# Attention units key group by key group, two weight splits moved, one opening half and one store moved, in a two-part transformer kernel

## The reference

```python
xn = rms_norm(h, mix_norm[l])
proj = einsum("bsd,dp->bsp", xn, w_in[l]) + b_in[l]
q, k, v, cb, cc, cx, ga, gc = split(proj, splits)
attn = sliding_window_attention(q, k, v, sinks[l])       # 8 heads of 64, 2 key groups, blocks of 128
conv = cb * causal_depthwise_conv(cc * cx, conv_w[l])
merged = sigmoid(ga) * (attn @ w_attn_branch) + sigmoid(gc) * (conv @ w_conv_branch)
h = h + merged @ w_out
hn = rms_norm(h, ffn_norm[l])                            # then up, conv, silu(gate)*val, down
...
return rms_norm_2(x, final_gain)                         # after the two hybrid layers
```

## Time and profile before

| | us |
|---|---|
| three runs, median | 1186.59 |
| the profiled execution | 1185.57 |
| its span, first to last instruction | 1183.8 |
| TensorE busy | 1172.0 |
| VectorE busy | 896.3 |
| ScalarE busy | 577.1 |
| GpSimd busy | 246.5 |

### The profile page before, as it was taken

The page is one execution under the profiler, slowest core; times in us unless marked ns, Lnnn a source line. Parts: engine busy times, 40 slices in busy tenths (PEclk is TensorE's granted clock), DMA queues, the critical chain, the costliest instruction groups (busy, mean ns, idle before and its releaser), DMA issues.

```text
span 1183.8 us, 14982 instructions
## 1 busy us (share of the span) xinstructions
PE 1172.0 (99%) x5539; PEld 983.4 (83%) x5539; DVE 896.3 (76%) x1482; ACT 577.1 (49%) x972; POOL 246.5 (21%) x223
## 2 busy tenths in 40 slices
PE   9999999999999999999999999999999999999997
PEld 7887788888888888888888888899888888898886
DVE  6889855656776487546776788997897878998876
ACT  6677623324343243325444477764335577753432
POOL 0220399931100000000003602101502311112200
PEclk9999999999999999999999999999999999999999
DMA  6455533333331533233332347663223376663521
GB/s 197 128 170 170 158 90 102 94 98 98 125 94 54 155 90 101 78 111 103 89 107 76 120 134 224 195 175 92 72 72 107 107 205 178 190 185 116 143 89 72
DMA packets 216717, 146.81 MB, mean 124 GB/s; under 512 B 6250, under 2 KB 205380, under 8 KB 216516
## 3 DMA queue, kind: packets, MB, share of 16 engines
q1 hardware_dynamic: 216628, 145.86, 42.3%
q10 hardware_dynamic: 16, 0.00, 0.0%
HBM read 127.49 MB, written 18.35 MB: 123 GB/s over the span
## 4 chain that ended last, share of the span: by engine, by line
PE 87%; DVE 7%; ACT 3%; issue 2%; DMA 1%; POOL 0%; DVEq 0%; SPq 0%; ACTq 0%
PE ps L191 86%; ACT a_p L161 1%; DVE tmp L164 1%; DVE wlo L164 1%; DVE a_p L178 1%; DVE a_pd L182 1%; DVE x1h L167 1%; DVE a_zc L167 0%; ACT whi L161 0%; DMA raw<-in_w_in_dram 0%; DMA xtm<-in_x_dram 0%; DVE smx L164 0%; ACT x1h L161 0%; PE ps L194 0%; DVE a_pt L164 0%
## 5 line engine op out<-in xcount | busy, mean ns | idle before, releaser
L161 ACT ACTIVATE whi<-raw 128x1024 fp32r<-128x1024 f32 (+2 forms) x199 | 206.9, 1045 | 293.5 <-PE ps L191 282.4
L164 DVE TENSOR_TENSOR wlo<-raw,whi 128x1024 fp32r<-128x1024 f32 (+2 forms) x193 | 252.1, 1311 | 43.7 <-ACT whi L161 43.2
L191 PE MATMUL ps<-x0h,whi 128*128 128x512 f32 x1008 | 254.8, 391 | 1.2 <-ACT whi L161 1.2
L191 PE MATMUL ps<-x0h,wlo 128*128 128x512 f32 x1008 | 254.4, 391 | 0.0
L191 PE MATMUL ps<-x0l,whi 128*128 128x512 f32 x1008 | 254.1, 390 | 0.0
L191 PEld LDWEIGHTS ps<-x0h,whi 128*128 128x128 f32 x1008 | 187.4, 188 | 39.6 <-ACT whi L161 1.5
L191 PEld LDWEIGHTS ps<-x0l,whi 128*128 128x128 f32 x1008 | 188.0, 188 | 38.8 <-DVE x0l L167 0.2
L191 PEld LDWEIGHTS ps<-x0h,wlo 128*128 128x128 f32 x1008 | 187.9, 188 | 38.4
L164 POOL TENSOR_TENSOR sums<-sums,sq 128x512 f32<-128x512 f32 x28 | 43.0, 1549 | 446.2 <-ACT sq L161 446.2
L191 PE MATMUL ps<-x1h,wlo 128*128 128x512 f32 x304 | 82.1, 389 | 0.0
L191 PE MATMUL ps<-x1l,whi 128*128 128x512 f32 x304 | 82.1, 389 | 0.0
(11 more groups left out here) (213 smaller groups left out, 1636.4 us busy)
## 6 DMA issues: line engine op xcount, KB each, us to landing
raw<-in_w_in_dram SPq DMA_DIRECT2D x98, 512.0 KB, 4.1
raw<-in_w_up_dram SPq DMA_DIRECT2D x44, 512.0 KB, 3.8
raw<-in_w_out_dram SPq DMA_DIRECT2D x24, 512.0 KB, 3.6
turned<-b_pd SPq DMA_DIRECT2D x16, 640.0 KB, 3.5
raw<-in_w_down_dram SPq DMA_DIRECT2D x16, 512.0 KB, 3.7
b_px<-turned SPq DMA_DIRECT2D x32, 160.0 KB, 3.4
b_p<-turned SPq DMA_DIRECT2D x32, 160.0 KB, 3.6
turned_a<-a_pd SPq DMA_DIRECT2D x6, 512.0 KB, 2.6
```

The source lines that it names most:

```text
L161: return AC.put(lambda e: e.activation(o, i, func, **kw), after, AC, 1)
L164: return on.put(lambda e: e.tensor_tensor(o, a, b, op), after, on, 1)
L191: return PE.put(lambda e: e.matmul(o, l, r, start=start, stop=stop), after, PE if mark else None, 1)
```

## The change

Four edits:
- Low halves of the convolution's cx and cb tiles go to GpSimd for j = 2 and 3; before for j = 0, 1 and 2. So tiles 6, 8, 9 and 11 move to VectorE, 15 and 17 to GpSimd, 12 and 14 stay there.
- In the opening the high half of the second feature tile is written by VectorE, and the low half of the first one comes behind it in VectorE's queue.
- The attention units are put on the agenda one query product sooner, all blocks of key group 0 and then those of group 1, at steps 3, 8, 12, 17, 21, 26, 30, 35 from there. The output bank and the DRAM buffer alternate by block instead of by group. The turning of the values uses bank 5 instead of 3.
- The first half of the last rows is stored from ScalarE's queue.

```diff
-                plan_fm(win, m, on_pool=j < 3 and n != 1)
+                plan_fm(win, m, on_pool=j > 1 and n != 1)
...
-            X0.th[k] = act(hi, PS[bank][:, :], scale=MIX(k), after=[tp, t_mix])
-            X0.tl[k] = stt(lo, PS[bank][:, :], MIX(k), f32(hi), ALU.mult, ALU.subtract, after=[tp, X0.th[k]])
+            if k == 1:
+                X0.th[k] = ts(hi, PS[bank][:, :], MIX(k), None, ALU.mult, after=[tp, t_mix])
+            else:
+                X0.th[k] = act(hi, PS[bank][:, :], scale=MIX(k), after=[tp, t_mix])
+
+            def low():
+                X0.tl[k] = stt(lo, PS[bank][:, :], MIX(k), f32(hi), ALU.mult, ALU.subtract, after=[tp, X0.th[k]])
+
+            if k:
+                if k == 1:
+                    lows.pop()()
+                low()
+            else:
+                lows.append(low)
...
-            free = claim(3)
+            free = claim(5)
...
-            u = (2 * n + g) % 2
+            u = n % 2
...
-            if j == 2:
-                for i, (n, g) in enumerate((n, g) for n in range(4) for g in range(2)):
-                    later(3 + 4 * i, unit_a(g, n))
+            if j == 1:
+                for i in range(8):
+                    later(3 + (9 * i + 1) // 2, unit_a(i // 4, i % 4))
...
-                t_done = dma(out[0][128 * t:128 * t + 128, 0:512], ob[:, t, 0:512], d_out, after=tf)
+                t_done = dma(out[0][128 * t:128 * t + 128, 0:512], ob[:, t, 0:512], d_out, after=tf, on=AC)
```

More of the change, by code:

```diff
@@ L574, in x_features @@
             return tp, rest
-        rests = {}
+        rests, lows = {}, []
         for c in range(4):
@@ L710, in evac_v @@
             yield 4
-            free = claim(3)
+            free = claim(5)
             for b in range(4):
-                tp = tr(PS[3][:, 128 * b:128 * b + 128], t[:, 128 * b:128 * b + 128], IDENT,
+                tp = tr(PS[5][:, 128 * b:128 * b + 128], t[:, 128 * b:128 * b + 128], IDENT,
                         after=[a, free], mark=b == 3)
@@ L716, in evac_v @@
             yield 1
-            src = PS[3][:, :].rearrange("p (b g d) -> p g b d", b=4, g=2)
+            src = PS[5][:, :].rearrange("p (b g d) -> p g b d", b=4, g=2)
             for g in range(2):
@@ L723, in evac_v @@
             vv_tok.extend([th, tl])
-            bank_free[3] = [th, tl]
+            bank_free[5] = [th, tl]
         def evac_q(j):
```

## The result

The kernel after takes 1192.33 us (median of six runs, 1191.32 to 1194.42), the kernel before 1186.19 in the runs beside it (1185.67 to 1187.21). The ratio is 1.0052, 95% interval 1.0039 to 1.0065: slower by 6.1 us, where +1.2 was forecast, and outside the range. The profiled execution took 1192.26 us, 6.7 more than that of before; its span is 1190.5.

A forecast was written before the change was run, and what follows sets the result against it. The prediction took VectorE's queue, not TensorE, to set the attention stage's end. It summed +1.4 (stage) + 0 - 0.2 (last rows) = +1.2 us on a 1186.59 us median to 1187.8 us, range 1184.0 to 1191.0.

The forecast's parts named there:

- The first unit's scores: Attention stage, step 3: TensorE waits for the second query tile's low halves, due at 44.0, losing 3.6 us (2.4 to 3.8).
- third query tile's low halves: Sign on VectorE in the attention stage: these low halves return to 0.77 us each.
- Waits for a_pt remain after 100 us: Sign on TensorE late in the attention stage: waits for the turned probabilities remain, 2 to 5 us in all.
- The tail: Storing the last rows: the second issue starts earlier with the first on ScalarE, -0.2 us (-0.48 to +0.33).
- three waits, not four: Attention stage before the change: TensorE was said to wait four times for a_pt between 33 and 125 us, 3.3 us in all.
- So the stage ends 1.4 us later.: Attention stage: VectorE's queue at the sixth unit's low half, 2.44 - 3.46 + 2.4 = +1.4 us (-0.5 to +3.2).
- the late waits' 4.1: Attention stage before: TensorE's waits for a_pt cost 1.76 + 2.35 = 4.1 us, the most the stage could gain.
- The term that was left to a rival: the clock: First unit: the gap drops TensorE's clock, two steps cost +3.6 us on top of the forecast, 1191.4 us; chance 0.08.
- a clock below 1.00 near 44 us: Sign near the first unit: the forecast is wrong if the granted clock falls below 1.00 there.
- GpSimd's remaining splits all hit: Rival, attention stage: all four GpSimd splits stretch VectorE's two-input operations, +4.5 us there, 1190.9 us; chance 0.28.
- x of 1.2: VectorE's loss beside each of two new GpSimd splits: 1.2 us, the mean of four seen, between 0 and 2.13.
- nothing for the opening: Opening: moving a high half from ScalarE to VectorE was costed at nothing, bounds -0.35 to +0.35 us.

The follow-up runs named there:

- gap filled: The kernel after with nine extra matmuls, result unused, ahead of the second pair of the first unit's waiting scores: 1190.35 us, ratio 1.0039.
- units at 6 + 4i: The kernel after with the first unit started three steps later and units 4 steps apart: 1187.70 us, ratio 1.0009.
- opening filled: The kernel before with two extra matmuls, result unused, ahead of the first weight product: 1186.43 us, ratio 1.0000.
- after with the old opening: The kernel after with the opening of before: 1191.12 us, ratio 1.0043.
- units alone: The kernel before with only the new schedule, bank and buffer of the attention units: 1189.97 us, ratio 1.0029.
- opening only: The kernel before with the opening edit alone: 1186.33 us, ratio 1.0005.
- nothing on GpSimd: The kernel after with all low halves of the convolution's tiles on VectorE: 1189.16 us, ratio 1.0026.
- units from step 5: The kernel before with after's units at steps 5 to 34 and GpSimd splitting only tiles 6, 11, 12 and 14: 1184.17 us, ratio 0.9986.

## Why the prediction was wrong

**What held.** The first unit's scores lost 3.68 us against a forecast of 3.6, the low halves being done at 45.11, or 43.87 without the opening's shift, against 44.0. The third query tile's low halves are back at 0.77 each. Waits for a_pt remain after 100 us, 3.6 us in all. The tail is worth nothing: the issue came sooner as worked out, but the two transfers then took longer. The opening edit costs nothing measurable by itself. One reading was off without effect: the earlier trace rows show three waits, not four.

**The step that failed: "So the stage ends 1.4 us later."** The forecast took VectorE's queue as what sets the end, as if its operations stood at fixed times, and let the first unit's 3.6 us vanish in the late waits' 4.1. But VectorE's queue is itself tied to TensorE: each scaling waits for a product. While TensorE stood still VectorE, rid of its two stretched low halves, got ahead, and then it waited 1.98 us for the delayed fourth query product (52.80). The chain of waits runs over TensorE for 13.95 us from 45.25 on, and VectorE fell behind afresh over the next units. So the first wait and the late waits add: rest 0.03 in the kernel after, the same when 1.6 us are given back early (gap filled), and only 0.8 more when the first unit's 5.3 are taken away (units at 6 + 4i). The chain of before had misled: it leaves TensorE out, but by little. The scaling of a convolution product comes at 58.77 us, 0.8 us after TensorE had gone on to what follows (57.97), and in the same kernel with its opening filled the chain runs over TensorE right up to that product. A TensorE that is 5 us late could hardly hide there. The line of VectorE's timeline in the kernel before:

```profile
58.77 0.68 DVE L164 TENSOR_TENSOR tmp<-ps,rb 128x512 f32<-128x512 f32 x1
```

**The term that was left to a rival: the clock.** The forecast gave 0.08 to a fall at the first unit. It fell in each of the five profiled kernels that had that gap unfilled, and cost 1.3 to 1.7 us in four of them and 2.8 in the fifth, without splits on GpSimd, where the second group of the product was slow as well. The place and the sign were right in the rival, its price of 3.6 too high, its chance far too low; a clock below 1.00 near 44 us was also among the prediction's own signs of being wrong (0.50 from 46 to 48 us). The forecast took the late gaps of 1.0 us as the measure, and this gap was 2.2. The page TensorE: Matmul & The Clock Gate, section Part 1: The HAM clock gate, of the Trainium skill has throttled as the default that activity releases; the 0.50 behind the gap, and 1.00 with the gap filled, agree.

**The rival "GpSimd's remaining splits all hit" was right in its mechanism.** All four stretch an operation with two SBUF inputs, by 1.30 to 2.10 us. The page SBUF — State Buffer, section Who interferes with whom, of the Trainium skill states that such an operation contends with a GpSimd instruction that reads SBUF; the trace agrees. So the forecast's x of 1.2 was too small: the two new splits (97.88 and 110.17) cost 2.10 and 1.31, and the two that stayed 1.82 and 1.30 instead of 1.1 and 0.4. The forecast's own sum then gives 2.44 - 3.46 + 3.4 + 1.6 = +4.0 us of VectorE's time instead of +1.4, near the rival's +4.5. How much of it reached the end isn't shown: nothing in the old order (1185.91 against 1186.07); beside the new one 0.9 us by the medians, not clear of the noise (after with the old opening against units alone). With none of the four the kernel after is 3.2 us faster.

**The sum, then.** 1.24 opening + 3.68 + 1.66 + 0.03 = 6.6 us of the 6.7 between the two profiled executions. With nothing for the opening it would be 5.4, and the medians differ by 6.1. The 3.68 was forecast well but taken as hidden, the 1.66 was left to a rival; these two make up 5.3 of the 6.6.

**What stays open.** Whether the opening edit makes the fall there likelier. The profiles show the fall in three of five kernels with the edit (after, gap filled, units at 6 + 4i; not opening only, nothing on GpSimd) and in one of six without it, where no extra matmuls stand in the opening. Taking it out, or filling the gap, gave 1.2 and 0.6 us in the median, and each time the clock fell later in the stage instead. Nor was it separated why units from step 5 shorten the late waits; the choice of GpSimd's tiles is not it, since without any the rest is nearly as short. And why the parts together cost some 2 us more than apart is known by place only.

## What to carry to other kernels

Before a new early wait is set off against later ones, look whether the late engine would come to wait for the other anywhere between; here it did, and the waits added. A gap on TensorE can cost more than its length, as the 1.3 to 2.8 us of slow matmuls behind this one show, so work that is begun sooner should not be begun before its inputs: three steps later alone gave back 4.6 of the 6.1 us. A split moved to GpSimd is to be priced by what VectorE does beside it, and not only by what it takes off VectorE's queue.

## What the runs showed that was not expected

- The same wait of 1.0 us on TensorE at the sixth unit left the clock at 1.00 in the profile of before and was followed by 0.57 (124 to 128 us) in that of the opening-only kernel; behind 2.03 to 2.06 us it fell in two kernels of five. One profile says what can happen behind a wait, not what does.
- In the opening it fell in four of thirteen changed kernels' profiles and in that of none with extra matmuls there; it cost 1.2 to 1.3 us of the third query product's start.
- Nine matmuls whose result nothing uses made a kernel faster, by 1.5 us in the profile and 2.0 in the median.
